# Silu by the hyperbolic tangent, joint splits of two heads, and other places for weight splits in the first attention

## The chip, the cores and the metric

The kernel runs on one core of a Trainium2 chip. The metric is the device time of one execution in microseconds (us), as the median of several. The engines are PE (TensorE, matrix products and transposes), DVE (VectorE), ACT (ScalarE), POOL (GpSimd) and SP (SyncE, which here only issues DMAs). Each engine runs its own instructions in program order, and semaphores order them between engines.

## What is computed

Two transformer blocks on 512 tokens of width 1024, all in float32. The change lies in the first block, whose core is this (projections by one matrix, two attentions with 8 heads each, gates by silu, an output projection and the sum with the input):

```python
proj = jnp.einsum('bsd,de->bse', xn, w_in[layer])
qa, ka, va, za, qi, ki, wi, qb, kb, vb, zb = jnp.split(proj, split_points, axis=-1)
...
a_out = dsa_attention(qa, ka, va, qi, ki, wi, bias_a)
b_out = dilated_attention(qb, kb, vb, bias_b)
mixed = jnp.concatenate([a_out.reshape(b, s, D_A) * jax.nn.silu(za),
                         b_out.reshape(b, s, D_B) * jax.nn.silu(zb)], axis=-1)
x = x + jnp.einsum('bse,ed->bsd', mixed, w_out[layer])
```

Attention a keeps, for each query, the best 128 keys of an index score; attention b is three dilated windows, here one causal softmax with a bias that counts how often a key is seen. The second block follows and isn't touched.

## The kernel before

Every float32 product is made of three products of halves: each operand is split into a high half (ACT copies it into a tile of type float32r, which rounds it) and a low half (the rest, by a subtraction on DVE or POOL), and PE adds high by high, high by low and low by high. So each operand passes through ACT and DVE before PE can use it.

The first attention is a loop over 64 steps, taken as pairs t, t+1. A step u is one token tile i (128 queries), one branch and one head; a group of 8 steps is two heads r = 0, 1 with i = 0, 1, 2, 3, branch b first (steps 0 to 31), then a (32 to 63). For the pair t, t+1 the engines do:

- PE: the scores of the pair (`pair1`, line 1086; at a group's start those of two pairs), then one or more chunks of the gate projection (`fill`), which are the other work of this stretch, then the transposes of the pair t-4 (`turn1`, line 1096), and at two places of each group the products with the values (`value1`, line 1111). Before each turn PE waits until the scores of the pair before are taken (`l_done`).
- DVE: `score1` (line 2269: bias, maximum, the score out of PSUM) for both steps, with a reciprocal of the sums of the pair before in between, which waits for that pair's exponentials; then, where a table says so, sums of values (`collect1`), the product of gate and attention (`mix`), the scaling of a finished gate tile (`gate_rows`), low halves of mixed rows (`mixed_low`), of gate weights (`low`, line 2090) and of output weights (`wo_low`); and last the low halves of the turned scores (`turned_low`, line 2222), which free the transpose bank (`t_free`).
- ACT: the high halves of the turned scores of the pair t-4 (`turned_high`, line 1761), the exponentials of the pair (`exps`, line 1578), low rows of the values' sums (line 1768), then the silus of two gate tiles (`silu`, line 1752), the high half of gate weights (`high`, line 1613), output weights (`wo_high`) and mixed rows (`mixed_high`), by the same kind of table.
- POOL: the scores times the reciprocal of their sum (line 2752), low halves of the values of branch a, the mask sums `combine` (line 2739), which `score1` needs in branch a, and a few low halves of output weights (line 2746).

The gate projection has eight tiles, zb 0 to 3 and za 0 to 3 (`FILL1`), with the weights in units F0 to F0+7 of 128x1024. A unit's raw weights have two places, so SP loads unit F0+2 only once PE has finished the tile F0, and so on. `HIGH1` and `LOW1` say at which step ACT and DVE split a unit: for F0+2 to F0+7 the high halves are at steps 10, 20, 28, 36, 43, 49, and the low ones at 12, 22, 30, 38, 44, 50; the low half of F0+1 is at step 1. `SILU_AT` has a pair of silus at steps 20, 36, 49 and 63. Two banks of PSUM take the transposes by turns (`t_bank`: tile n waits until tile n-2 is freed); each step is a tile of its own.

## Time and profile before

| | |
|---|---|
| median of 3 timed runs | 1031.36 us (1031.04 to 1031.43) |
| the profiled execution | 1029.16 us, of which 1027.3 us is the span from first to last instruction |
| granted TensorE clock | 0.999 of full speed |
| PE busy | 1005.7 us, 98% |
| DVE busy | 680.4 us, 66% |
| ACT busy | 563.2 us, 55% |
| POOL busy | 422.8 us, 41% |
| first attention | about 170 to 303 us of the span |

The profile is of one execution; its times are those of all rows below. An engine's rows give the start in the span, the length, the line of the kernel, and in brackets the idle time ahead of it with the instruction that ended it. A matmul's length runs past the start of the next, since they are pipelined. An engine is the bound where the others wait for it; idle time of others costs nothing by itself.

### The profile page before, as it was taken

To read this page: it belongs to the slowest core of one execution; us is meant where nothing else is said; L and a number is where in the kernel's file an instruction comes from. 1 tells how busy PE (TensorE), PEld (TensorE's weight loads), DVE (VectorE), ACT (ScalarE), POOL (GpSimd) and SP (SyncE) were. 2 spreads that over 40 slices of the span, in tenths; PEclk is the share of its full clock that TensorE was granted. 3 is DMA by queue.
4 is the path that set the end of the run, shared out by engine and by line. 5 is a ranking of instruction groups with operands and counts; after the bars stand their busy time and mean duration, and the time that the engine had idled before them with its cause. 6 is when DMAs were issued, how large, how long until landed. Compare 5 with 4: busy or idle time off the path is not lost. (4 is left out here: it accounts for less than half of the span.)

```text
span 1027.3 us, 14257 instructions
## 1 busy us (share of the span) xinstructions
PE 1005.7 (98%) x5150; PEld 826.2 (80%) x5150; DVE 680.4 (66%) x1207; ACT 563.2 (55%) x1032; POOL 422.8 (41%) x407
## 2 busy tenths in 40 slices
PE   9999999999989999999999999999999999999997
PEld 7788877777778898878887788888888888888885
DVE  5578997788974446824567879454322325999997
ACT  8455445778873355544567884234433446554564
POOL 0024011557840002900264430007779965874562
PEclk9999999999999999999999999999999999999999
DMA  9433321336140384233200362239999941443552
GB/s 336 104 98 109 88 67 36 83 83 191 56 175 1 103 267 143 60 82 83 63 2 1 121 229 62 82 111 323 347 352 349 356 168 62 153 143 135 205 185 82
DMA packets 100166, 146.25 MB, mean 142 GB/s; under 512 B 6480, under 2 KB 60496, under 8 KB 100096
## 3 DMA queue, kind: packets, MB, share of 16 engines
q1 hardware_dynamic: 86800, 130.75, 38.9%
q10 hardware_dynamic: 12768, 12.88, 4.0%
q0 software_dynamic: 528, 1.70, 0.9%
q8 instruction: 41, 0.67, 0.3%
q14 instruction: 29, 0.24, 0.1%
HBM read 123.69 MB, written 21.63 MB: 141 GB/s over the span
## 5 line engine op out<-in xcount | busy, mean ns | idle before, releaser
L2578 DVE TENSOR_TENSOR w_lo<-wring,w_hi 128x1024 fp32r<-128x1024 f32 x32 | 51.4, 1607 | 107.5 <-ACT w_hi L1944 107.5
L2090 DVE TENSOR_TENSOR u_lo<-wring,u_hi 128x1024 fp32r<-128x1024 f32 (+1 forms) x64 | 82.5, 1296 | 53.6 <-ACT u_hi L1613 52.9
L935 PE MATMUL bank<-u_hi,h_hi 128*128 128x512 f32 (+1 forms) x288 | 110.9, 385 | 0.1
L935 PE MATMUL bank<-u_hi,h_lo 128*128 128x512 f32 (+1 forms) x288 | 109.3, 379 | 0.0
L935 PE MATMUL bank<-u_lo,h_hi 128*128 128x512 f32 (+1 forms) x288 | 109.0, 378 | 0.0
L1613 ACT ACTIVATE u_hi<-wring 128x1024 fp32r<-128x1024 f32 (+1 forms) x64 | 66.2, 1034 | 69.4 <-PE bank L935 54.7
L935 PE MATMUL bank<-h_hi,w_hi 128*128 128x512 f32 (+2 forms) x272 | 103.2, 379 | 0.0
L935 PE MATMUL bank<-h_hi,w_lo 128*128 128x512 f32 (+2 forms) x272 | 103.1, 379 | 0.0
L935 PE MATMUL bank<-h_lo,w_hi 128*128 128x512 f32 (+2 forms) x272 | 103.1, 379 | 0.0
L935 PE MATMUL bank<-h_hi,u_hi 128*128 128x512 f32 x224 | 93.8, 419 | 0.4 <-ACT arena L1555 0.2
L1441 PE MATMUL bank<-s_hi,f_hi 128*128 128x512 f32 x224 | 87.4, 390 | 0.7 <-DVE f_lo L2612 0.7
L935 PE MATMUL bank<-h_lo,u_hi 128*128 128x512 f32 x224 | 87.7, 391 | 0.0
L935 PE MATMUL bank<-h_hi,u_lo 128*128 128x512 f32 x224 | 87.7, 391 | 0.0
L1442 PE MATMUL bank<-s_hi,f_lo 128*128 128x512 f32 x224 | 87.2, 389 | 0.0
L1443 PE MATMUL bank<-s_lo,f_hi 128*128 128x512 f32 x224 | 87.2, 389 | 0.0
L1944 ACT ACTIVATE w_hi<-wring 128x1024 fp32r<-128x1024 f32 x32 | 33.9, 1060 | 91.9 <-PE bank L935 91.9
L2804 POOL TENSOR_SCALAR arena<-arena,stats 128x128 f32<-128x128 f32 (+3 forms) x64 | 40.5, 642 | 95.0 <-DVE stats L2534 94.8
L2752 POOL TENSOR_SCALAR x<-x,stats 128x128 f32<-128x128 f32 (+3 forms) x64 | 49.4, 777 | 53.9 <-DVE stats L2277 53.9
L2604 DVE TENSOR_TENSOR s_lo<-wring,s_hi 128x2048 fp32r<-128x2048 f32 (+1 forms) x32 | 67.8, 2119 | 5.6 <-ACT s_hi L1974 5.6
L935 PEld LDWEIGHTS bank<-u_hi,h_hi 128*128 128x128 f32 x288 | 54.1, 188 | 11.5 <-issue 1.2
L935 PEld LDWEIGHTS bank<-u_lo,h_hi 128*128 128x128 f32 x288 | 54.1, 188 | 10.2
L1974 ACT ACTIVATE s_hi<-wring 128x2048 fp32r<-128x2048 f32 (+1 forms) x32 | 54.3, 1696 | 14.0 <-PE bank L1443 13.8
(382 smaller groups left out, 2600.2 us busy)
## 6 DMA issues: line engine op xcount, KB each, us to landing
wring<-in_w_in SPq DMA_DIRECT2D x60, 512.0 KB, 3.9
wring<-in_w_ff ACTq DMA_DIRECT2D x12, 1024.0 KB, 8.7
wring<-sums_kept SPq DMA_DIRECT2D x16, 768.0 KB, 4.2
wring<-in_w_ff SPq DMA_DIRECT2D x22, 512.0 KB, 6.2
wring<-in_w_ff SPq DMA_DIRECT2D x32, 256.0 KB, 3.3
sums_kept<-wring SPq DMA_DIRECT2D x22, 256.0 KB, 5.2
wring<-in_w_out SPq DMA_DIRECT2D x2, 2048.0 KB, 13.2
wring<-in_w_ff SPq DMA_DIRECT2D x4, 1024.0 KB, 6.9
```

Source lines behind the costliest of these rows:

```text
L935: last = mm(b, lhs, rhs, start=(start and n == 0), stop=(stop and n == 2))
L1441: mm(b, f[0][:, token], w[0][:, high], start=start, stop=False)
L1442: mm(b, f[1][:, token], w[0][:, high], start=False, stop=False)
L1443: return mm(b, f[0][:, token], w[1][:, lows], start=False, stop=stop)
L1613: run(u_hi[hi_place(u)][:, 0:unit_cols(u)], raw_unit(u), ACT.Copy).then_inc(u_hi_done, 1)
L1944: run(dst, src, ACT.Copy).then_inc(w_hi_done, 1)
L1974: run(s_hi[m % 4][:, 0:PAIR - at], pair_raw(m)[:, at:PAIR], ACT.Copy).then_inc(s_hi_done, 1)
L2090: v.tensor_tensor(u_lo[raw_place(u)][:, 0:cols], raw_unit(u), u_hi[hi_place(u)][:, 0:cols].bitcast(F32), ALU.subtract).then_inc(u_lo_done, 1)
L2578: v.tensor_tensor(cut(w_lo[ring3(m)]), src, cut(w_hi[ring3(m)]).bitcast(F32), ALU.subtract).then_inc(w_lo_done, 1)
L2604: v.tensor_tensor(s_lo[pair_place(m)][:, at:PAIR], pair_raw(m)[:, at:PAIR], s_hi[m % 4][:, 0:PAIR - at].bitcast(F32), ALU.subtract)
L2752: g.tensor_scalar(logits1[u % 8], logits1[u % 8], den[:, u:u + 1], unit_factor, ALU.mult, ALU.mult).then_inc(scaled, 1)
L2804: g.tensor_scalar(place, place, den2[:, u:u + 1], gates[:, i, at:at + 1], ALU.mult, ALU.mult).then_inc(scaled, 1)
```

## The change

The silu z * sigmoid(z) is written as 0.5 * z * (1 + tanh(z/2)). ACT makes tanh(z/2) (`half_tanh`), and in a second pass adds 1; POOL multiplies by z (`gated`); the factor 0.5 goes into DVE's product `mix`. The eight tiles are taken one by one (`TANH_AT`, `GATED_AT`) instead of in four pairs, and the exponential's table is loaded ahead of the attention. For token tiles 0 and 1 the turned scores of both heads lie in one bank and are split by one ACT and one DVE instruction (`turned_high_pair`, `turned_low_pair`), and such a pair counts as one tile of the two banks. The high halves of F0+2 to F0+7 are at steps 9, 19, 27, 35, 41, 47. The low halves of F0+1, F0+3, F0+4 and F0+6 are done in two parts at two steps. Some of DVE's `mix` are at other steps.

```diff
@@ -198,12 +198,14 @@
-    HIGH1 = {filled[tile] + 2: unit_of[tile] + 2 for tile in FILL1 if unit_of[tile] + 2 < U2}
-    LOW1 = {1: F0 + 1, **{step // 2 * 2 + 2: u for step, u in HIGH1.items()}}
+    HIGH1 = {filled[tile] // 2 * 2 + 1: unit_of[tile] + 2 for tile in FILL1 if unit_of[tile] + 2 < U2}
+    LOW1 = {4: (F0 + 1, 0), 6: (F0 + 1, 1), 10: (F0 + 2, None), 20: (F0 + 3, 0), 22: (F0 + 3, 1), 28: (F0 + 4, 0), 30: (F0 + 4, 1),
+            38: (F0 + 5, None), 42: (F0 + 6, 0), 46: (F0 + 6, 1), 50: (F0 + 7, None)}
...
-    SILU_AT = {min(filled[FILL1[2 * n + 1]] + 2, NS - 1) if n < 3 else NS - 1: n for n in range(4)}
-    MIX_AT = {22: 0, 24: 1, 38: 2, 40: 3, 50: 4, 56: 5, 64: 6}
+    TANH_AT = {10: 0, 20: 1, 28: 2, 36: 3, 42: 4, 48: 5, 54: 6, 60: 7}
+    GATED_AT = {12: 0, 21: 1, 29: 2, 37: 3, 45: 4, 53: 5, 61: 6, 62: 7}
+    MIX_AT = {18: 0, 32: 1, 34: 2, 40: 3, 50: 4, 56: 5, 64: 6}
...
-    T1 += [("pt", u) for u in range(NS)]
+    T1 += [("pt", u) for u in range(NS) if steps1[u][0] >= 2 or u % 2 == 1]
...
+    TT.update({("pt", u): TT[("pt", u + 1)] for u in range(0, NS, 2) if steps1[u][0] < 2})
...
+        pt1_both = {part: half(f"pt1_pair_{part}", 6 * P, ("wring", pt1_at[0, part, 0])) for part in ("hi", "lo")}
...
@@ -1091,10 +1112,11 @@
-                b = t_bank(("pt", u))
+                b, at = t_bank(("pt", u)), (i + 1) * P * (u % 2) if i < 2 else 0
...
-                last.then_inc(t_full, 1)
+                if i >= 2 or u % 2 == 1:
+                    last.then_inc(t_full, 1)
...
+                if g == "qa":
+                    nc.scalar.preload_act_table(ACT.Exp)
...
-            def silu(tile):
+            def half_tanh(tile):
                 act.wait_ge(a_free, AT[tile] + 1)
-                z = zT[:, (0 if tile[0] == "za" else 4) + tile[1], :]
-                run(z, z, ACT.Silu).then_inc(z_done, 1)
+                act.wait_ge(l_done, (0 if tile[0] == "zb" else HALF) + NH * (tile[1] + 1))
+                run(tanh_place(tile), gate_place(tile), ACT.Tanh, scale=0.5).then_inc(half_tanh_done, 1)
+                act.wait_ge(half_tanh_done, FILL1.index(tile) + 1)
+                run(tanh_place(tile), tanh_place(tile), ACT.Identity, bias=unit_factor).then_inc(tanh_done, 1)
+
+            def turned_high_pair(u):
+                i, o = steps1[u][0], u // NH
+                k = TT[("pt", u)]
+                act.wait_ge(t_full, k + 1)
+                if o >= 1:
+                    act.wait_ge(pv_done, 4 * (o - 1) + 2)
+                run(both_places("hi", i), pair_turned(k, i), ACT.Copy).then_inc(pt_hi_done, 2)
...
-                        for n in range(2):
-                            silu(FILL1[2 * SILU_AT[u] + n])
+                    if u in TANH_AT:
+                        half_tanh(FILL1[TANH_AT[u]])
...
+            def turned_low_pair(u):
+                i = steps1[u][0]
+                dve.wait_ge(pt_hi_done, u + 2)
+                v.tensor_tensor(both_places("lo", i), pair_turned(TT[("pt", u)], i), both_places("hi", i).bitcast(F32), ALU.subtract)\
+                    .then_inc(t_free, 1)
...
-                v.tensor_tensor(zT[:, k, cols], zT[:, k, cols], qk1[:, o // 4, o % 4, OUTS, cols], ALU.mult).then_inc(gated_done, 1)
+                v.scalar_tensor_tensor(zT[:, k, cols], zT[:, k, cols], 0.5, qk1[:, o // 4, o % 4, OUTS, cols], ALU.mult, ALU.mult)\
+                    .then_inc(gated_done, 1)
...
+            def gated(tile):
+                pool.wait_ge(tanh_done, FILL1.index(tile) + 1)
+                z = gate_place(tile)
+                g.tensor_tensor(z, z, tanh_place(tile), ALU.mult).then_inc(z_done, 1)
...
+                if u in GATED_AT:
+                    gated(FILL1[GATED_AT[u]])
```

The order on ACT around step 20, in the program before. `x,stats<-x,stats` is a pair of exponentials, `pt1_hi...` a turned copy, `arena<-arena` a silu, `u_hi3` the high half of unit F0+3:

```order
L1578 ACTIVATE x,stats<-x,stats 128x384 x2
L1752 ACT_TABLE_LOAD
L1752 ACTIVATE arena<-arena 128x512 x2
L1613 ACTIVATE u_hi3_90<-wring 128x1024
L1761 ACTIVATE pt1_hi00_118<-bank4 128x2x128
L1761 ACTIVATE pt1_hi01_119<-bank5 128x2x128
L1578 ACT_TABLE_LOAD
L1578 ACTIVATE x,stats<-x,stats 128x512 x2
```

The same place in the program after; line 1776 is the tanh, 1778 the second pass, 1754 a mixed high half:

```order
L1635 ACTIVATE u_hi3_90<-wring 128x1024
L1786 ACTIVATE pt1_pair_hi_118<-bank4 128x2x128
L1600 ACTIVATE x,stats<-x,stats 128x384 x2
L1776 ACTIVATE arena<-arena 128x512
L1778 ACTIVATE arena<-arena,stats 128x512
L1754 ACTIVATE qk1_half_103<-arena 128x512
L1786 ACTIVATE pt1_pair_hi_118<-bank5 128x2x2x128
L1600 ACTIVATE x,stats<-x,stats 128x512 x2
```

The loads are gone, one silu is two passes, the weights' high half stands a turn earlier, and the turned scores of a pair are one copy.

ACT around steps 40 to 43, before, where `u_hi2` is the high half of unit F0+6:

```order
L1761 ACTIVATE pt1_hi11_115<-bank5 128x3x128
L1578 ACTIVATE x,stats<-x,stats 128x128 x2
L1730 ACTIVATE qk1_half_103<-arena 128x512
L1761 ACTIVATE pt1_hi10_114<-bank4 128x4x128
L1761 ACTIVATE pt1_hi11_115<-bank5 128x4x128
L1578 ACTIVATE x,stats<-x,stats 128x256 x2
L1768 ACTIVATE consts<-bank6 64x512
L1613 ACTIVATE u_hi2_89<-wring 128x1024
```

And after:

```order
L1795 ACTIVATE pt1_hi11_115<-bank5 128x3x128
L1600 ACTIVATE x,stats<-x,stats 128x128 x2
L1635 ACTIVATE u_hi2_89<-wring 128x1024
L1795 ACTIVATE pt1_hi10_114<-bank4 128x4x128
L1795 ACTIVATE pt1_hi11_115<-bank5 128x4x128
L1600 ACTIVATE x,stats<-x,stats 128x256 x2
L1802 ACTIVATE consts<-bank6 64x512
L1776 ACTIVATE arena<-arena 128x512
```

The high half of F0+6, which waits for its DMA, has moved ahead of the turned copies of steps 38 and 39.

## Rows read from the trace of the kernel before

**Rows 1.** The page's first part: busy time, share of the span, instructions.

```profile
PE 1005.7 (98%) x5150; PEld 826.2 (80%) x5150; DVE 680.4 (66%) x1207; ACT 563.2 (55%) x1032; POOL 422.8 (41%) x407
```

**Rows 2.** Who PE waited for, 168 to 300 us: total, times, longest.

```profile
PE bank L1096 <- DVE pt_lo L2222: 4.5, 6, 1.3
PE bank L1086 <- DVE stats L2269: 3.9, 6, 1.4
```

**Rows 3.** Order of time, PE: start, length, instruction, idle before it.

```profile
175.24 0.79 PE L1086 MATMUL bank<-qk_half 64*128 64x384 f32 x6 [1.18 <-DVE stats L2269]
...
193.96 0.95 PE L1086 MATMUL bank<-qk_half 64*128 64x128 f32 x12 [0.71 <-DVE stats L2269]
...
209.83 0.85 PE L1096 MATMUL bank<-consts,x 128*128 128x128 f32 x6 [0.89 <-DVE pt_lo L2222]
...
214.18 1.09 PE L1096 MATMUL bank<-consts,x 128*128 128x128 f32 x8 [0.52 <-DVE pt_lo L2222]
...
244.75 1.10 PE L1096 MATMUL bank<-consts,x 128*128 128x128 f32 x8 [0.37 <-DVE pt_lo L2222]
...
248.09 0.38 PE L1096 MATMUL bank<-consts,x 128*128 128x128 f32 x2
...
254.81 0.96 PE L1086 MATMUL bank<-qk_half 64*128 64x128 f32 x12 [1.39 <-DVE stats L2269]
...
265.89 0.30 PE L1096 MATMUL bank<-consts,x 128*128 128x128 f32 x1 [1.05 <-DVE pt_lo L2222]
...
292.37 1.09 PE L1096 MATMUL bank<-consts,x 128*128 128x128 f32 x8 [1.35 <-DVE pt_lo L2222]
```

**Rows 4.** Order of time, ACT at step 20.

```profile
204.43 1.28 ACT L1752 ACT_TABLE_LOAD   x1
...
206.78 1.04 ACT L1613 ACTIVATE u_hi<-wring 128x1024 fp32r<-128x1024 f32 x1
...
208.38 1.28 ACT L1578 ACT_TABLE_LOAD   x1
```

**Rows 5.** Groups by line and shape, ACT, 168 to 300 us: count, busy, mean ns.

```profile
L1761 ACT ACTIVATE pt_hi<-bank 128x512 fp32r<-128x512 f32 x16 | 8.7, 593 | 11.8 <-PE bank L1096 11.8
...
L1761 ACT ACTIVATE pt_hi<-bank 128x256 fp32r<-128x256 f32 x16 | 5.2, 378 | 7.3 <-PE bank L1096 7.3
...
L1752 ACT ACT_TABLE_LOAD x4 | 5.1, 1283 | 0.1
...
L1752 ACT ACTIVATE arena<-arena 128x512 f32<-128x512 f32 x8 | 4.6, 624 | 0.0
```

**Rows 6.** Loads of units F0+2 and F0+6 (issue, then KB and us to landing), ACT beside them.

```profile
182.14 0.37 SPq L739 DMA_DIRECT2D wring<-in_w_in  x1
...
wring<-in_w_in SPq DMA_DIRECT2D x1, 512.0 KB, 4.6
...
186.23 1.09 ACT L1761 ACTIVATE pt_hi<-bank 128x512 fp32r<-128x512 f32 x2 [2.13 <-PE bank L1096]
...
240.75 0.42 SPq L739 DMA_DIRECT2D wring<-in_w_in  x1
...
wring<-in_w_in SPq DMA_DIRECT2D x1, 512.0 KB, 7.4
...
245.41 1.09 ACT L1761 ACTIVATE pt_hi<-bank 128x512 fp32r<-128x512 f32 x2 [1.47 <-PE bank L1096]
...
248.20 1.06 ACT L1613 ACTIVATE u_hi<-wring 128x1024 fp32r<-128x1024 f32 x1
```

**Rows 7.** POOL: a group by shape, two rows in time, busy time from 280 to 290.

```profile
L2739 POOL TENSOR_TENSOR junk<-arena,x 128x512 f32<-128x512 f32 x8 | 10.3, 1285 | 0.0
...
257.91 2.80 POOL L2752 TENSOR_SCALAR x<-x,stats 128x512 f32<-128x512 f32 x1
...
286.96 2.90 POOL L2752 TENSOR_SCALAR x<-x,stats 128x384 f32<-128x384 f32 x4
...
280.00:290.00 10.00, 9.04 (x61) 7.32 (x57) 7.53 (x22) 8.95 (x24) 9.51 (x12) 1.00 0.01 2
```

More of the change, by code:

```diff
@@ L444, in build, with both_places, pair_turned @@
         assert sum(pt1_size[key[0]] for key in pt1_at) == 5 * UNIT
-        pt1 = {key: half(f"pt1_{key[1]}{key[0]}{key[2]}", 2 * (2 * key[0] + 2) * P, ("wring", at)) for key, at in pt1_at.items()}
+        pt1 = {key: half(f"pt1_{key[1]}{key[0]}{key[2]}", 8 * P, ("wring", at)) for key, at in pt1_at.items() if key[0] == 1}
+        pt1_both = {part: half(f"pt1_pair_{part}", 6 * P, ("wring", pt1_at[0, part, 0])) for part in ("hi", "lo")}
+        pt1.update({(0, part, r): pt1_both[part][:, 3 * P * r:3 * P * (r + 1)] for part in pt1_both for r in range(2)})
+        pt1_pair = {part: both[:, :].rearrange("p (r m s) -> p r m s", r=2, s=P) for part, both in pt1_both.items()}
+        def both_places(part, i):
+            return pt1_pair[part][:, :, 1:2, :] if i == 0 else pt1_pair[part][:, :, 0:3:2, :]
+        def pair_turned(k, i):
+            return bank[4 + k % 2][:, 0:2 * (i + 1) * P].rearrange("p (r m s) -> p r m s", r=2, s=P)
         def turned_place(part, i, r):
@@ L453, in build, with gate_place, tanh_place @@
         mix_place = lambda k: (0, k - 4) if k >= 4 else (1, k)
+        def gate_place(tile):
+            return zT[:, (0 if tile[0] == "za" else 4) + tile[1], :]
+        def tanh_place(tile):
+            return qk1[:, 0 if tile[0] == "zb" else 1, tile[1], MIX_LO, :]
         def wo_raw(n, k, count=1):
@@ L555, in build @@
         ki_lo_done = sem("ki_lo_done")
+        half_tanh_done = sem("half_tanh_done")
+        tanh_done = sem("tanh_done")
         z_done = sem("z_done")
@@ L1093, in turn1 @@
                 pe.wait_ge(scaled, u + 1)
-                b = t_bank(("pt", u))
+                b, at = t_bank(("pt", u)), (i + 1) * P * (u % 2) if i < 2 else 0
                 for j in range(i + 1):
-                    last = nc.tensor.transpose(b[:, (i - j) * P:(i - j + 1) * P], logits1[u % 8][:, j * P:(j + 1) * P], ident)
-                last.then_inc(t_full, 1)
+                    last = nc.tensor.transpose(b[:, at + (i - j) * P:at + (i - j + 1) * P], logits1[u % 8][:, j * P:(j + 1) * P], ident)
+                if i >= 2 or u % 2 == 1:
+                    last.then_inc(t_full, 1)
             def value1(o, n, r):
@@ L1770, in _ @@
             for t in range(0, NS + 4, 2):
-                if t >= 4:
+                if t >= 4 and steps1[t - 4][0] < 2:
+                    turned_high_pair(t - 4)
+                elif t >= 4:
                     turned_high(t - 4)
@@ L2084, in head_low, with low @@
                                        small[:, gain:gain + 1], place[:, :, hi, :].bitcast(F32), ALU.mult, ALU.subtract).then_inc(t_free, 1)
-            def low(u):
+            def low(u, part=None):
                 dve.wait_ge(u_hi_done, u + 1)
-                cols = unit_cols(u)
-                v.tensor_tensor(u_lo[raw_place(u)][:, 0:cols], raw_unit(u),
-                                u_hi[hi_place(u)][:, 0:cols].bitcast(F32), ALU.subtract).then_inc(u_lo_done, 1)
+                size = unit_cols(u) // (1 if part is None else 2)
+                cols = slice((part or 0) * size, (part or 0) * size + size)
+                done = v.tensor_tensor(u_lo[raw_place(u)][:, cols], raw_unit(u)[:, cols],
+                                       u_hi[hi_place(u)][:, cols].bitcast(F32), ALU.subtract)
+                if part != 0:
+                    done.then_inc(u_lo_done, 1)
             def branch_low(e):
@@ L2298, in _ @@
                     if u in LOW1:
-                        low(LOW1[u])
+                        low(*LOW1[u])
                     if WO_HIGH.get(u - 2, 5) < 5:
                         wo_low(WO_HIGH[u - 2])
-                if t >= 4:
+                if t >= 4 and steps1[t - 4][0] < 2:
+                    turned_low_pair(t - 4)
+                elif t >= 4:
                     turned_low(t - 4)
@@ L2747, in output_low @@
                     .then_inc(wo_lo_done, 1)
+            def gated(tile):
+                pool.wait_ge(tanh_done, FILL1.index(tile) + 1)
+                z = gate_place(tile)
+                g.tensor_tensor(z, z, tanh_place(tile), ALU.mult).then_inc(z_done, 1)
             for u in range(NS):
```

2 lines of the change are left out of this document (removed).

## The prediction

> **What bounds the kernel now.** The page first: PE is busy 98% of the span [rows 1], so only time in which PE stands still, or is fed late, can be won, and the change touches nothing but the first attention (170 to 303 us). Next, who PE waits for in that stretch. Two entries lead: the transposes (line 1096) wait for the low split of an earlier turned tile, 4.5 us, and the score products (line 1086) for the score step of DVE, 3.9 us [rows 2]. Then the order of time on PE: rows 3 has the stalls, the time in brackets being the stall. I number the work by the step u of the loop (a pair t, t+1 per turn). They are, in order: the scores of step 4 (1.18) and of step 16 (0.71), the transposes of steps 20 (0.89), 22 (0.52) and 38 (0.37), the scores of step 48 (1.39), the transposes of step 48 (1.05) and of step 62 (1.35). The row without a stall, at 248.09, is the transposes of step 40.
>
> Last, what ACT does ahead of them [rows 4]. At step 20 it loads a table, runs two silus, makes a high half of a weight tile, splits step 18, and loads the exponential's table again: 204.43 to 209.66, 5.2 us, where the loads alone are 2.6. PE's stall at 209.83 is the far end of it: the transposes need a bank that DVE's low split frees, and that split comes behind ACT's copy and DVE's own low half of the weights. So PE is the bound, and ACT and DVE, in turns, set its gaps.
>
> **The change, part by part.** Times below are in the coordinates of the trace of before; "+x" is how much later than there PE stands.
>
> *Tables.* Line 1752 has four loads of 1283 ns [rows 5], and line 1578 as many, one of them at the very start and one behind each of the first three silu pairs [rows 4]. The program after has none between the exponentials and one before the attention, where ACT waits for PE anyway: 8 x 1.28 = 10.3 us leave ACT in this stretch. Added are eight Identity passes (about 0.62 to 0.7 us, from a silu's 624 ns [rows 5]) = 5.3 us, so ACT gets 5.0 us back. POOL gets eight products of 128x512; its 128x512 sum takes 1285 ns [rows 7], so 10.3 us.
>
> A load stands right behind the instruction before it and the next right behind it, 1.28 us in all [rows 4]. The Trainium skill, "ScalarE: Activation LUTs", section "What ACT_TABLE_LOAD costs", gives 1283 ns and another 1380 ns of drain, 2.66 us per switch. The first half agrees with the trace; the drain isn't seen in it. By that rule ACT would get 21.3 us instead of 10.3; I take the row.
>
> *Joint splits.* For 16 pairs (token tiles 0 and 1) two copies of ACT become one. Two copies of 128x256 take 2 x 378 ns, one of 128x512 593 ns [rows 5]: 0.16 us less for each of 8 pairs. The 128-wide pairs, not shown, I put at as much (bounds 0 and 0.4). DVE's halves shrink likewise. More useful is that a pair takes one transpose bank, so the first head of the next pair waits for a split that is one pair older.
>
> *Step 4.* The 1.18 us wait is for scores 3, behind the reciprocal which waits for ACT's exponentials (late by one load), and behind a whole low half. Both go: no load, and the low half is now at steps 4 and 6, where DVE stood waiting for ACT. The next thing, ACT's two exponentials, ends before PE asks. -1.2.
>
> *Steps 8 to 16.* The high half of the third gate tile (u_hi for step unit F0+2) moves from the turn of step 10 to that of step 8. Its DMA is issued at 182.14 and lands 4.6 us later, at 186.74 [rows 6]. ACT reaches the place at 184.1, so it now stands in front of the turned copies of step 6, which began at 186.23 [rows 6]; they begin at 186.74 + 1.05 = 187.8. DVE does the low half to 189.0, then the splits of 6 and 7 to 189.65 and 190.3. PE wants the first one's bank at 188.77: 0.9 lost. On the other side the low half, which stood ahead of the splits of step 8 and the scores of 14 and 15 and caused most of the 0.71 at step 16, is gone from there. Following ACT (copies, exponentials, low rows, tanh and Identity, joint copy, exponentials) the scores of step 15 end at 194.2 and PE goes on at 194.35 instead of 193.96. +0.4 (bounds -0.5 and +1.5).
>
> *Step 20.* ACT: the high half now comes one turn earlier, its DMA has landed by then (asked for 4 us before, and nothing else in flight). Exponentials end at 205.6, tanh, Identity and a mixed-high copy at 207.45, joint copy of step 18 at 208.0, instead of 208.37. DVE holds only half of a low half and one mixed-low there and frees the bank at 209.45; PE wants it at 209.2 for its second head. PE stands at 209.2 instead of 209.83, from +0.4 to -0.6: -1.0.
>
> *Steps 22 to 26.* The 0.52 us came from the same backlog, and so did, by my reading, 0.6 in the value products and scores right behind (the same rows stand that much closer together in the groups before): -1.1 (bounds -0.5 and -1.2). What stays is a wait of 0.2 to 0.3 at each group's start, where scores need a whole turn from PE to DVE and back.
>
> Up to step 32 PE is then 2.9 us ahead, and nothing in the rows stops it till step 38.
>
> *Steps 38 to 48, the seventh gate tile.* This is the term that decides. The 0.37 at step 38 goes (ACT is 1 us ahead there). But the high half of unit F0+6 moves from step 43 to step 41. Its load is queued behind eight strip loads and two megabyte loads; it is issued at 240.75 and takes 7.4 us: 248.15 [rows 6]. Before, ACT came to it at 248.20, so it had no slack at all [rows 6]. Now ACT comes to it at 242.3 and stands 5.8 us; queued behind it are the turned copies of step 38, which ran at 245.41 [rows 6]. All of this chain hangs on PE's own progress, so the gain so far moves the landing as well. High half to 249.2, copies to 250.25; DVE's split of 38 to 250.5 (a half low half is ahead of it); PE's transposes of step 40, which ran at 248.09 [rows 3], start at 250.55: +2.45. From there: score 47 at 256.25 (its mask sum on POOL at 255.45), PE goes on at step 48 at 256.35 instead of 254.81 [rows 3]. The 1.39 wait of before is inside that, so the net is +1.6 (bounds 0 and +3.5: the landing is uncertain by one, and one more megabyte load is now issued some 1 us earlier beside it).
>
> *Steps 48 to 53.* ACT has two weight copies of 128x1024, the high half of the last tile, whose DMA, issued at 255.2 by this walk, lands by 259.8 at the price of the third tile's, and then the turned copies: they end at 262.4, DVE's at 263.95. PE loses 0.4, 0.6 and 0.95 (1.95) where it lost 1.35 before, the 1.05 and 0.30 on the pair's second head; since its products behind close up again, I take +0.3 (bounds 0 and +0.6). *Steps 54 to 56*: POOL's chain of scale and mask sum waits for a reciprocal 0.3 later: +0.3.
>
> *The end.* The last silus stood ahead of the splits of steps 60 to 63 (PE's 1.35). They go, but POOL now has two products between the scalings of steps 61, 62 and 63, and it is in one piece there: scalings from 286.96 to 289.82 [rows 7]. With 2 x 1.29 more the last scaling ends at 292.4, and PE wants it about 291.4 for the second head. 1.0 stays of the 1.35 and a smaller wait of 0.5 behind it: -0.8.
>
> **Sum:** -1.2 + 0.4 - 1.0 - 1.1 + 1.6 + 0.3 + 0.3 - 0.8 = -1.5 us. The profiled execution took 1029.16 us, 1027.30 of it span; it is 2.2 below the median of the three timed runs, 1031.36. A difference of PE time carries over to either, so I forecast 1031.36 - 1.5 = 1029.9 us.
>
> **Rivals.** *A, the seventh tile doesn't hold ACT* (its load lands by 243 to 244, since what is ahead in the queues is gone by then). For it: the third tile's load took 4.6 us [rows 6]. Against it: this one took 7.4 with the same company. Then 0.4 at step 38, 1.2 of the 1.39 and 1.3 of the 1.35 at step 48 go too: -2.9 - 0.4 - 1.2 - 1.3 - 0.8 = -6.6, and 0.4 in the value products behind step 62: -7.0, 1024.4 us.
>
> *B, POOL becomes the pacemaker and it gets slower.* One 128x512 scaling, 0.77 elsewhere, took 2.80 us at 257.91 while DVE subtracted two weight tiles [rows 7], and between 280 and 290 POOL was busy 9.51 of 10 us [rows 7]. If the products of steps 53, 61 and 62, where it has no room, take 2.8 instead of 1.29, that is 3 x 1.5 = 4.5 us more in front of PE: 1029.9 + 4.5 = 1034.4. It decides from about 2.5 us per product (3 x 1.2 = 3.6: 2.1 over the time of before). Against it: the mean of the mask sums, the same shape, was 1.285 [rows 7]. The Trainium skill, "SBUF — State Buffer", section "Who interferes with whom", has a DVE instruction with two SBUF inputs and a GpSimd one that reads SBUF block each other for a whole instruction; the 2.80 agrees with that.
>
> *C, the gain isn't there*: PE's gaps close but it waits for scores instead, each turn of PE and DVE being near its own limit; 1031.4, within 1 either way. For it: the wait at each group's start, which no part of the change shortens.
>
> **How the numbers follow.** Forecast case 0.58, with a spread of about 2 us from its bounds: 0.24 below -2.1, 0.32 within, 0.02 above. A 0.18, B 0.16, C 0.08 (0.05 of it within, 0.03 slower, if the waits for scores are longer than the gaps). A measurement of this kernel tells about 0.2% (2.1 us) from no change. Faster by over 0.2%: 0.24 + 0.18 = 0.42. Slower: 0.02 + 0.16 + 0.03 = 0.21. Within: 0.37. Range 1024.4 to 1033.6; it cuts off the far half of A and of B. Both signs hold much, so the likeliest case alone: 1027.5 to 1031.5.
>
> **What would show it.** On PE: no stall at step 4; transposes of steps 20 to 22 without one; a stall of 2 to 3 us at step 40's transposes, and ahead of it ACT idle some 5 us, released by a DMA into wring, before line 1635. If that idle is under 1 us, A is right. A second, shorter one of that kind (2.5 us) at step 8. If POOL's products (line 2799) average over 2 us and PE's stalls move to the scaled tiles from step 45 on, B. I'm wrong altogether if the landing of the seventh tile moves, or if ACT's copies overtake it.

## The result, and the profile after

The change made the kernel slower. In nine runs each, the kernel after has a median of 1037.20 us (1033.90 to 1039.78), the kernel before 1031.43 (1031.03 to 1034.08); the ratio is 1.0044, 95% interval 1.003 to 1.0058. On another chip (e12 below) it was 1.003 (1.0017 to 1.0042). I had forecast 1029.9 in a range of 1024.4 to 1033.6. The profiled execution took 1034.49 us, 1032.7 of it span: 5.4 us longer than before, and 5.05 of that is there when the first attention ends. The nine runs fall in two groups: four of 1033.90 to 1034.49, three of them with a granted clock of 0.998 over the span and one with 0.995, and five of 1037.20 to 1039.78 with 0.993 to 0.995. The profile is of the first group; none was taken of the second, so where its clock fell isn't known.

The page's first part, which answers to [rows 1]:

```profile
PE 1007.4 (98%) x5150; PEld 827.8 (80%) x5150; DVE 681.1 (66%) x1195; ACT 559.7 (54%) x1017; POOL 437.0 (42%) x415
```

Who PE waited for from 168 to 306 us, which answers to [rows 2] (total, times, longest):

```profile
PE bank L1117 <- DVE pt_lo L2266: 5.2, 4, 1.9
PE bank L1117 <- DVE pt_pair_lo L2259: 3.5, 3, 1.7
PE bank L1107 <- DVE stats L2314: 1.5, 4, 0.7
PE bank L956 <- DVE u_lo L2126: 1.4, 1, 1.4
```

The work did shift as intended: ACT is 3.5 us less busy, POOL 14.2 more. The waits for scores are down from 3.9 us to 1.5, but those of the transposes (line 1117, which was 1096) rose from 4.5 to 8.7: 5.2 for single low splits and 3.5 for joint ones (line 2259), and there is a new one for gate weights (line 2126). In order of time on PE, which answers to [rows 3]:

```profile
174.43 0.79 PE L1107 MATMUL bank<-qk_half 64*128 64x384 f32 x6
...
189.00 0.42 PE L1117 MATMUL bank<-consts,x 128*128 128x128 f32 x2 [0.76 <-DVE pt_lo L2266]
...
210.84 0.52 PE L1117 MATMUL bank<-consts,x 128*128 128x128 f32 x3 [1.73 <-DVE pt_pair_lo L2259]
...
240.99 0.52 PE L1117 MATMUL bank<-consts,x 128*128 128x128 f32 x3 [1.02 <-DVE pt_pair_lo L2259]
...
249.75 0.42 PE L1117 MATMUL bank<-consts,x 128*128 128x128 f32 x2 [1.38 <-DVE pt_lo L2266]
...
255.76 0.96 PE L1107 MATMUL bank<-qk_half 64*128 64x128 f32 x12 [0.73 <-DVE stats L2314]
...
258.11 0.50 PE L956 MATMUL bank<-h_hi,u_hi 128*128 128x512 f32 x1 [1.39 <-DVE u_lo L2126]
...
296.07 1.09 PE L1117 MATMUL bank<-consts,x 128*128 128x128 f32 x8 [1.90 <-DVE pt_lo L2266]
```

The stall at step 4 is gone (174.43). Four places are new or worse. The first two are transposes of a pair's second head, at step 20 (210.84) and step 36 (240.99). This is what DVE and POOL did ahead of them:

```profile
207.65 1.29 POOL L2799 TENSOR_TENSOR arena<-arena 128x512 f32<-128x512 f32 x1
...
207.75 1.74 DVE L2299 TENSOR_TENSOR qk_half<-arena,qk_half 128x512 fp32r<-128x512 f32 x1 [0.88 <-ACT qk_half L1754]
...
237.43 1.73 POOL L2799 TENSOR_TENSOR arena<-arena 128x512 f32<-128x512 f32 x1
...
237.93 2.32 DVE L2126 TENSOR_TENSOR u_lo<-wring,u_hi 128x1024 fp32r<-128x1024 f32 x1
```

DVE's mixed-low took 1.74 us, and ended 0.55 behind the end of POOL's product (208.94); the same subtraction takes 0.69 elsewhere. The low half of unit F0+5 took 2.32 instead of 1.21 (e3 below, which has no such product beside it). The same happens once more ahead of the 1.39 at 258.11, with the product of step 45 and the second part of the low half of F0+6:

```profile
256.23 1.27 POOL L2799 TENSOR_TENSOR arena<-arena 128x512 f32<-128x512 f32 x1
...
256.29 1.76 DVE L2126 TENSOR_TENSOR u_lo<-wring,u_hi 128x512 fp32r<-128x512 f32 x1
```

This subtraction of 128x512 takes 0.68 in e3, and PE doesn't wait behind it there. Third, ACT stands in front of the high half of F0+6, and later in front of the last tanh:

```profile
247.21 1.06 ACT L1635 ACTIVATE u_hi<-wring 128x1024 fp32r<-128x1024 f32 x1 [4.40 <-DMA wring<-in_w_in]
...
288.79 0.63 ACT L1776 ACTIVATE arena<-arena 128x512 f32<-128x512 f32 x1 [2.12 <-DVE stats L2314]
```

Fourth, behind the stall of 1.90, the granted clock. In each row of the windows: the window and its length in us, busy time (count) of PE, PEld (PE's weight loads), DVE, ACT, POOL, then the granted clock as a share of 2.4 GHz, the DMA share and GB/s.

```profile
294.00:296.00 2.00, 0.17 (x1) 0.00 (x0) 1.97 (x4) 0.71 (x2) 2.00 (x2) 1.00 0.00 0
296.00:298.00 2.00, 1.60 (x10) 1.32 (x11) 1.95 (x5) 1.26 (x3) 1.92 (x3) 0.98 0.00 0
298.00:300.00 2.00, 2.00 (x10) 1.72 (x8) 2.00 (x4) 1.69 (x4) 1.47 (x2) 0.50 0.68 244
300.00:302.00 2.00, 2.00 (x12) 1.95 (x12) 1.47 (x2) 0.14 (x1) 0.59 (x1) 0.66 1.03 414
```

PE had 0.17 us of work in 294 to 296, and from 298 it ran at half clock (1.2 GHz) for over 3 us. The kernel before has 1.00 in this stretch. e3 (below) has the same wait for the last tanh and keeps its clock at 1.00, and it loses 1.7 there instead of 2.8; it also has next to no products, so at most some 1.1 of the 2.8 goes with the clock.

**Where the time went.** For each kernel, PE's start of the same instruction less that in the trace of before, as the change in each stretch. The stretches end, in the time of before, at the scores of step 4 (175), the scores of step 16 (194), the value products behind step 22 (218), the transposes of step 38 (245), fill products behind step 48 (259), score products at 280, and the end of the attention (303). An offset of 0.3 to 3.2 us that each execution brings along from ahead of the attention is taken off. Each row is one profiled execution; the medians of the timed runs stand with the experiments. "half" marks a stretch with the clock at half in part. The experiments of the later rows follow below.

```
                    to 175  194   218   245   259       280   303       sum
predicted            -1.2  +0.4  -2.1   0    +1.6      +0.6  -0.8      -1.5
after                -1.2  +0.5  -0.2  +0.8  +2.2      -0.2  +2.8 half +4.6
e12 after again      -1.2  +0.3  -0.3  +0.8  +3.8 half -1.8  +2.5 half +4.0
e1 late tanh         -1.2  +0.3  -2.1  +0.7  +5.2 half +1.0  +0.2      +4.1
e2 F0+6 back         -1.2  +0.3  -0.4  +0.7  +0.1      -0.2  +2.8 half +2.2
e3 no product        -1.3  +0.5  -2.2  -0.4  +4.4 half +1.4  +1.7      +4.1
e4 late, F0+6 back   -1.2  +0.4  -0.2  +0.7  +0.1      -0.2  +0.2      -0.1
e5 product at 23     -1.3  +0.2  -1.4  +0.8  +1.7 half -1.7  +0.2      -1.6
e6 F0+2 back         -1.2  +0.2  -2.1  +0.7  +1.8 half -1.8  +1.7 half -0.8
e7 old silus         -1.3  +0.2  +0.2  +0.3  +0.1      +0.3  +0.2      +0.1
e8 joint only         0.0  +0.1  -0.3   0.0   0.0       0.0  +0.2      +0.1
e9 e6, product at 23 -1.2  +0.2  -2.1  +0.7  +0.2      -0.2  +1.7 half -0.7
e10 low F0+5 split   -1.3  +0.2  -1.5  -0.1  +1.7 half -1.8  +1.7 half -1.0
e11 end reordered    -1.3  +0.2  -2.1  -0.1  +0.1      -0.1  -0.1      -3.4
```

### The profile page after: what moved, and what is told of

Its sections match the earlier page's. It is cut to its first block and busy times, and to the rows that moved or that the text cites. A ratio compares the mean times of both kernels' runs of the same rounds, so it can differ in the third digit from the quotient of the medians.

```text
span 1032.7 us, 14234 instructions
## 1 busy us (share of the span) xinstructions
PE 1007.4 (98%) x5150; PEld 827.8 (80%) x5150; DVE 681.1 (66%) x1195; ACT 559.7 (54%) x1017; POOL 437.0 (42%) x415
## 5 line engine op out<-in xcount | busy, mean ns | idle before, releaser
L2126 DVE TENSOR_TENSOR u_lo<-wring,u_hi 128x1024 fp32r<-128x1024 f32 (+2 forms) x68 | 85.0, 1257 | 57.5 <-ACT u_hi L1635 56.8
L956 PEld LDWEIGHTS bank<-u_hi,h_lo 128*128 128x128 f32 x288 | 54.1, 188 | 9.3
```

The costliest lines, as they stand in the source:

```text
L956: last = mm(b, lhs, rhs, start=(start and n == 0), stop=(stop and n == 2))
L2126: done = v.tensor_tensor(u_lo[raw_place(u)][:, cols], raw_unit(u)[:, cols], u_hi[hi_place(u)][:, cols].bitcast(F32), ALU.subtract)
```

## The experiments

The ratios are to the kernel before on the same chip, with 95% intervals; each batch of four (e1 to e4, e5 to e8, e9 to e12) shared a chip. The kernel after ran on the chip of the last batch alone, so what is said of e1 to e8 against it, and of kernels of different batches against each other, compares ratios across chips.

### e1, e2 and e4: the two largest losses

e1 moves the last tanh behind the last exponentials:

```diff
-    TANH_AT = {..., 54: 6, 60: 7}
-    GATED_AT = {..., 53: 5, 61: 6, 62: 7}
+    TANH_AT = {..., 54: 6, 62: 7}
+    GATED_AT = {..., 53: 5, 61: 6, 63: 7}
```

> The changed kernel with one edit: the tanh of the last gate tile and its second pass at step 62 instead of 60 (behind the exponentials of steps 62 and 63), its product on POOL at step 63 instead of 62. The changed kernel lost 5.4 us of span, about 2.9 of it behind 280 us: ACT stood 2.12 us there because this tanh waits until all scores are taken. Theory 1 (this wait starves PE, and PE's clock falls to half behind it): ACT's idle time ahead of line 1776 goes, the transposes of step 62 wait under 1 us, the granted clock stays at 1.00 from 290 to 303, and the drift of PE against the kernel before at the end of the attention falls from 5.05 to about 2.2; median 1033.7 to 1034.7, and no run above 1036 if the spread of the changed kernel's runs (1033.9 to 1039.8) came from this place. Rival (POOL's two products at the end are what holds PE): POOL has the same work, so PE waits as long for the scaled scores; within 0.5 us of the changed kernel.

e2 puts the seventh gate tile's weights back:

```diff
+    HIGH1[43] = HIGH1.pop(41)
...
-    LOW1 = {..., 42: (F0 + 6, 0), 46: (F0 + 6, 1), 50: (F0 + 7, None)}
+    LOW1 = {..., 44: (F0 + 6, None), 50: (F0 + 7, None)}
```

> The changed kernel with the seventh gate tile's weights as before: high half of unit F0+6 at step 43 instead of 41, low half whole at step 44 instead of in two parts at 42 and 46. Theory 1 (the early high half held ACT 4.4 us for its DMA, cost PE 1.4 at the transposes of step 40 and, through the late second low part, 1.39 at 258.11): both PE stalls go, the drift of PE at 270 us falls from about +2.0 to between 0 and +0.5; time 1.5 to 2.3 us below the changed kernel, if nothing later eats it. Rival (the wait of 1.39 for the scores of step 48 takes both in, as in the kernel before): 0.5 us or less below. The clock fall at 297 to 301 stays in either.

e4 is both edits together.

> The edits of the two kernels above together: last tanh at step 62, its product at 63, and the seventh gate tile's weights as before. Theory 1 (two separate places): the gains add, 4.3 to 5 us below the changed kernel in its profile, so about 1031 to 1032.5, level with the kernel before. Rival (the places are not independent: what is won at 258 is waited for again at the end): the gain is that of the first alone, some 2.8 us, 1033.5 or more.

**Measured:** before 1030.71; e1 1031.79, ratio 1.0008 (0.9993 to 1.0024); e2 1031.71, 1.0005 (0.9993 to 1.0017); e4 1029.40, 0.9984 (0.9972 to 0.9996). Against the kernel after (1.0044, 1.003) each edit alone wins 2 to 4 us, and both together 5 to 6: theory 1 holds for both places. In the profiles e4 is 4.7 us below the kernel after, which is the 2.6 that e1 wins in the last stretch and the 2.1 that e2 wins before 259; by the medians the sum of the single gains is 5 to 8, so there they add up only roughly.

In e1's profile (1033.25 us, in the upper part of its runs of 1028.91 to 1036.20) the last stretch costs 0.2 us instead of 2.8, and the clock stays at 1.00 there; the transposes of step 62 wait 0.40. But one part of the expectation missed: a run above 1036 was left (1036.20). The clock can fall at the other gap too, and in this profile all but 0.5 us of what e1 wins at the end and at step 20 is lost there. e1's ACT and PE around the high half of F0+6, in order of time:

```profile
246.82 1.06 ACT L1635 ACTIVATE u_hi<-wring 128x1024 fp32r<-128x1024 f32 x1 [6.03 <-DMA wring<-in_w_in]
...
249.35 0.66 PE L1117 MATMUL bank<-consts,x 128*128 128x128 f32 x2 [2.99 <-DVE pt_lo L2266]
```

And its windows (columns as above):

```profile
246.00:248.00 2.00, 0.36 (x2) 0.00 (x0) 0.09 (x1) 1.18 (x2) 0.20 (x1) 1.00 0.47 171
248.00:250.00 2.00, 0.65 (x3) 0.68 (x4) 2.00 (x4) 1.98 (x7) 0.00 (x0) 0.61 0.03 11
250.00:252.00 2.00, 2.00 (x12) 2.00 (x11) 1.56 (x7) 1.97 (x4) 1.55 (x2) 0.50 0.00 0
252.00:254.00 2.00, 2.00 (x11) 1.68 (x12) 1.03 (x2) 1.81 (x6) 2.00 (x3) 0.50 0.00 0
254.00:256.00 2.00, 2.00 (x10) 1.22 (x7) 0.86 (x4) 0.00 (x0) 0.55 (x1) 0.69 0.00 0
```

PE was 2.0 us earlier here than in the kernel after (transposes of step 38 at 243.02 instead of 245.03), yet those of step 40 start at 249.35 instead of 249.75. The load lands at 246.8 instead of 247.2. Its issue in the kernel after, then in e1:

```profile
240.51 0.42 SPq L760 DMA_DIRECT2D wring<-in_w_in  x1
```

```profile
239.34 0.42 SPq L760 DMA_DIRECT2D wring<-in_w_in  x1
```

It was issued 1.2 us earlier and took 7.5 us instead of 6.7; the DMA share is 0.98 to 1.19 in every window from 236 to 246, with strips and megabyte loads issued ahead of it. That doesn't make the landing fixed. With each execution's offset taken off, it comes at 246.8 in the kernel after, 246.5 in e12, 246.2 in e1, 245.3 in e3, and 244.5 to 245.0 in e6, e9 and e11, whose PE is as far ahead as e1's at 236 (3.1 us against 3.0; 0.9 in the kernel after). Over the fourteen profiles the landing is about 1 us earlier for each us that PE is ahead there, with a scatter of 0.6, and the load takes 6.5 to 8.1 us. So e1 had the slower load of the two: by the same count PE is 2.2 us ahead of the kernel after at step 38, the landing 0.6, and 1.6 of the lead is waited away in front of step 40. The longer gap then brings the clock down. In e2 ACT comes to the tile at 249.05, 0.9 us behind its landing, with no wait at all, and the stretch costs 0.1 instead of 2.2.

The end of e4 shows what is next there, a low half of the output weights that POOL makes behind the last product:

```profile
292.22 1.09 PE L1117 MATMUL bank<-consts,x 128*128 128x128 f32 x8 [0.41 <-DVE pt_lo L2266]
294.86 0.70 PE L956 MATMUL bank<-za_half,qk_half 128*128 128x512 f32 x2 [1.54 <-POOL qk_half L2793]
```

### e3, e5, e6, e9: POOL's products, and a race at step 20

e3 takes nearly all of the products away. It leaves out 510 of the 512 columns of each, so its gates are not the right ones; it is for the time alone:

```diff
-                g.tensor_tensor(z, z, tanh_place(tile), ALU.mult).then_inc(z_done, 1)
+                g.tensor_tensor(z[:, 0:2], z[:, 0:2], tanh_place(tile)[:, 0:2], ALU.mult).then_inc(z_done, 1)
```

> The changed kernel, but POOL multiplies only two of the 512 columns of each gate tile (line 2799 as 128x2 instead of 128x512), so most of the gate isn't multiplied by z. All waits stay. Theory 2 (a POOL product beside a DVE subtraction makes both longer, and the joint splits come late behind it): DVE's mixed-low at step 20, 1.74 us in the changed kernel, takes about 0.7, its low half of F0+5, 2.32, about 1.2; the stalls of 1.73 at step 20 and 1.02 at step 36 fall below 0.5 and the 1.39 at 258.11 shrinks; with POOL free at the end too the time falls by 3 to 5 us. Rival (ACT's second pass and its queue are the cause, DVE would wait for ACT anyway): the two stalls stay at over 1 us, and at most 1.5 us is won, at the end only.

**Measured:** 1035.34, ratio 1.0034 (1.0021 to 1.0046). By the ratios it is 1 us better than the kernel after was in its first series, and no better than in e12; 3 to 5 were expected. The collisions do go (F0+5's low half takes 1.21; the stretches to 218 and 245 win 2.0 and 1.2), and so does the wait of 1.39 for the gate weights:

```profile
257.35 0.68 DVE L2126 TENSOR_TENSOR u_lo<-wring,u_hi 128x512 fp32r<-128x512 f32 x1
```

But all of it is lost in front of F0+6's load: ACT waits 6.15 us there, PE 3.11, and the clock falls from 249 to 255. So the products cost 3.2 us up to step 38 and over 1 behind it, and without them the total is hardly better as long as F0+6 is split early. POOL as pacemaker (rival B) is out. What the products cost in a kernel with F0+6 at its old place wasn't run.

e3 alone doesn't show that the product costs PE time at step 20, though. e1 has the full products and shows the same gain there. Its DVE and POOL rows there:

```profile
206.29 2.25 POOL L2804 TENSOR_SCALAR x<-x,stats 128x384 f32<-128x384 f32 x2 [2.54 <-DVE stats L2322]
...
206.73 0.77 DVE L2299 TENSOR_TENSOR qk_half<-arena,qk_half 128x512 fp32r<-128x512 f32 x1
```

It is a race. If ACT's mixed-high is there when DVE has taken its scores, DVE goes first: its mixed-low takes 0.77, and POOL's two scalings are held (2.25 instead of 1.30). If DVE has to wait for ACT (0.88 in the kernel after), POOL's scalings and then its product come in between, and one of DVE's next two subtractions is held until the product ends: the mixed-low (1.74 and 1.87 in after and e4) or the low half behind it (1.77 in e12 and e2, where the mixed-low takes 0.83 and 0.79). With the product at step 21 PE lost 1.9, 1.7, 1.7 and 1.9 us (after, e12, e2, e4) or nothing (e1, e6) at the transposes of step 20, counted from the first head's start to the second's against the 0.33 us of a kernel without a stall. What seems to decide it stands a turn earlier, at the high half of unit F0+3, which the change put at step 19. In the kernels that lost, ACT waited there for its load (the kernel after, then e1):

```profile
203.24 1.06 ACT L1635 ACTIVATE u_hi<-wring 128x1024 fp32r<-128x1024 f32 x1 [0.79 <-DMA wring<-in_w_in]
```

```profile
202.26 1.04 ACT L1635 ACTIVATE u_hi<-wring 128x1024 fp32r<-128x1024 f32 x1
```

It is 0.79, 0.45, 0.50 and 0.68 us in after, e12, e2 and e4, where the load took 4.9 to 5.3 us, and nothing in e1 and e6, where it took 3.7 and 3.8. Of the kernels without a product at 21, e3, e9 and e11 had no such wait and lost nothing, e5 waited 0.59 and lost 0.6, and e10 is the exception: no wait, and yet DVE stood 0.22 us for ACT and PE lost 0.5. This is a correlation over eleven profiles; the high half of F0+3 alone wasn't moved.

e5 is e4 with the product moved:

```diff
-    GATED_AT = {12: 0, 21: 1, ...}
+    GATED_AT = {12: 0, 23: 1, ...}
```

> The kernel of e4_late_f6 with one number changed: POOL's product of the second gate tile at step 23 instead of 21. In e4_late_f6 this product (208.23 to 209.52) ran beside DVE's mixed-low of step 20, which took 1.87 us instead of 0.7, and PE lost 1.9 us at the transposes of step 20. Theory (a POOL product and a DVE subtraction of two SBUF operands take turns, and it is this collision that PE pays): the mixed-low takes 0.7 to 0.8, PE loses less than 0.9 there, and the time is 1.0 to 1.9 us below e4_late_f6 (ratio to the kernel before 0.9965 to 0.9975). Rival (DVE waits for ACT's mixed-high there anyway, 0.74 us, and POOL's scaled scores collide in the product's place): PE loses 1.5 us or more as before, and the time is within 0.4 us of e4_late_f6.

**Measured:** before 1031.01; e5 1028.87, ratio 0.9978 (0.9968 to 0.9987), 0.6 us better than e4 within overlapping intervals. The mixed-low takes 0.69 and PE loses 0.6 at step 20 instead of 1.9, as the theory had it; in its rows DVE stands 0.65 us for ACT there, which accounts for the 0.6. The time is between theory and rival, and its profile holds a clock fall at 255 that e4's doesn't. In four kernels with the product at 23 the loss was 0.6, 0, 0.5 and 0 (e5, e9, e10, e11), never 1.7.

e6 is e4 with the third gate tile's weights put back:

```diff
+    HIGH1[10] = HIGH1.pop(9)
-    LOW1 = {..., 10: (F0 + 2, None), ...}
+    LOW1 = {..., 12: (F0 + 2, None), ...}
```

> The kernel of e4_late_f6 with the third gate tile's weights as in the kernel before: high half of unit F0+2 at step 10 instead of 9, low half at 12 instead of 10. By the prediction's sum the early place costs 0.4 net: the stall of 0.66 at the transposes of step 8 goes (drift there 0.9 lower), and 0.5 of the wait at the scores of step 16 comes back; so 0.4 us below e4_late_f6 (0 to 0.8). Rival (the later place pushes ACT's and DVE's work of step 12 into the next turn): a stall of over 0.7 at step 16 or at 12's transposes, 0.3 us or more above it.

**Measured:** 1027.86, ratio 0.9974 (0.9964 to 0.9984): 1.0 us better than e4 by the ratios, within overlapping intervals, where I had put 0.4. The stall at step 8 is gone, and from step 4 to 16 it loses 0.2 instead of 0.4. The larger part, 1.9 at step 20 in its profile, is the race going the good way. Whether the later place of F0+2 makes that likelier I can't tell from one profile.

e9 is e6 with the product at 23.

> The kernel of e6_f2_back (last tanh at 62, the weights of the third and the seventh gate tile as in the kernel before) with POOL's product of the second gate tile at step 23 instead of 21. Reading so far: at step 20 POOL's scaled scores and product and DVE's mixed-low race for the same port; in the profile of e6_f2_back DVE came first and PE lost nothing there, so the later product can win nothing in such an execution. Theory (a race that goes one way or the other from one execution to the next): the profile shows the mixed-low at 0.7 to 0.8 and PE's loss at step 20 under 0.9 whichever comes first; median 0 to 0.7 us below e6_f2_back, 0.9970 (0.9963 to 0.9976) of the kernel before. Rival (the product at 23 meets other work of DVE): above 0.9978.

**Measured:** before 1031.07; e9 1028.81, ratio 0.9975 (0.9963 to 0.9987), the same as e6: the smallest gain that was expected, nothing where the race was won anyway.

### e7 and e8: the parts alone

e7 is e4 with the silus of the kernel before, in pairs at steps 20, 36, 49 and 63, and `mix` as it was.

> The kernel of e4_late_f6 with the silus of the kernel before: pairs by the silu table at steps 20, 36, 49 and 63, no second pass, no product on POOL, a plain product on DVE, and the products with the attention at the steps of before; joint splits and the places of the weight halves stay those of e4_late_f6. Theory (what the tables give back, the products on POOL take: 1.9 us at step 20 and 1.3 at step 36 lost to collisions): within 1 us of e4_late_f6, and PE's stalls at steps 20 to 22 are those of the kernel before (0.89 and 0.52) less what the joint splits and the earlier high half save. Rival (the table loads are the gain, as the prediction had it with 2.1 us at steps 20 to 26 and 0.8 at the end): 2 to 3 us above e4_late_f6, slower than the kernel before.

e8 has nothing of the change but the joint splits.

> The kernel before with the joint splits alone: the turned scores of both heads of token tiles 0 and 1 in one bank, split by one ACT and one DVE instruction; silus, tables and all weight halves as before. Theory (a pair takes one transpose bank, so the next pair waits for an older split): the stalls of 0.89 at step 20 and 1.35 at step 62 shrink by 0.3 to 0.5 each, 0.5 to 1.2 us below the kernel before. Rival (the bank of a pair is free only when both heads are split, so the second head waits longer): the stalls stay or grow, within 0.3 us of the kernel before or above it.

**Measured:** e7 1031.23, ratio 1.0001 (0.999 to 1.0012); e8 1031.40, 1.0002 (0.9992 to 1.0012). The joint splits alone give nothing, as the rival had it. In e8 the stall at step 20 moved from the first head (0.89 before) to the second:

```profile
209.37 0.49 PE L1117 MATMUL bank<-consts,x 128*128 128x128 f32 x3
210.69 0.52 PE L1117 MATMUL bank<-consts,x 128*128 128x128 f32 x3 [0.83 <-DVE pt_pair_lo L2259]
```

e7 is 1.7 us above e4 by the ratios, between theory and rival. Its profile says why: the stretch from step 16 to 22 costs +0.2 with the tables, and -2.1 with the tanh when the race is won, -0.2 when it is lost. So the silus by tanh (no loads, one tile at a time, other places for `mix`) are worth the 2.1 us that I had put there, and the product's collision can take nearly all of it. Which of the three gives it, e7 doesn't separate.

### e10 to e12: the better version, and the kernel after once more

```diff
-    LOW1 = {..., 38: (F0 + 5, None), ...}
+    LOW1 = {..., 36: (F0 + 5, 0), 38: (F0 + 5, 1), ...}
```

> The kernel of e9_f2_23 with the low half of unit F0+5 in two parts at steps 36 and 38 instead of whole at 38, where it took 2.3 us beside POOL's product and PE lost 1.2 at the transposes of step 38's turn. Theory: the part at 38 ends about 0.6 earlier, so the stall on the joint low split (L2259) near 241 shrinks from 1.26 to about 0.6; 0.5 to 0.7 us below e9_f2_23, part of it taken back by the scores' wait of step 48 (1.82). Rival (POOL's product holds DVE till it ends, whatever stands there): the stall stays above 1.0, nothing won.

**Measured:** 1027.21, ratio 0.9958 (0.9944 to 0.9972). The stretch to step 38 goes from +0.7 to -0.1 and the stall there is gone, a little more than expected (0.5 to 0.7); that the ratio is 1.7 us better than e9's is within overlapping intervals.

e11, on top of it:

```diff
-    WO_POOL = {59: 5, 63: 6}
+    WO_POOL = {59: 5}
...
                 if t == NS + 2:
                     collect1(GROUPS - 2)
-                    mix(7, slice(0, S // 2))
...
+                if t == NS - 2:
+                    dve.wait_ge(wo_lo_done, 6)
+                    wo_low(6)
+            mix(7, slice(0, S // 2))
             mixed_low(6)
```

> The kernel of e10_low5_split with two moves at the end of the attention: the low half of output weight 6 from POOL (behind the last product) to DVE at step 62, and DVE's first product of the last gate tile behind the splits of steps 62 and 63. In the kernels with the late tanh PE waits 1.54 us for that low half on POOL at the end. Theory (POOL's queue of two products and two low halves is what the last silu's table was before): this wait goes, the next one is that for the turned low split at about 0.5 us; 1.0 to 1.5 us below e10_low5_split, and fewer runs in which the clock falls behind it. Rival (DVE is as late with its splits as POOL with the weights): 0.4 us or less.

**Measured:** 1027.38, ratio 0.9964 (0.9953 to 0.9975). In the profile the 1.54 wait is gone, waits of 0.84 and 0.57 stand in its place, and the last stretch costs -0.1 instead of +0.2 (or +1.7 where the clock falls). The 1.0 to 1.5 us below e10 that were expected don't show: in time it isn't distinguishable from e10; e10's five runs against e11's twelve can't settle a microsecond. Both beat the kernel before by 3.7 to 4.3 us, and the kernel after, on the same chip (e12), by some 7.

> The changed kernel once more, on the chip of these runs. Theory: at the median 1.0044 (1.003 to 1.006) of the kernel before, with the same holding of ACT by the load of unit F0+6 (4 to 6.2 us) in its profile. What may differ from one execution to another is the collision at step 20 (mixed-low of DVE 0.75 or 1.75 us) and at which gap the granted clock falls to half (about 250 us, or 298 us, or both): spans fall into groups some 2 us apart. Rival (the collision and the clock's falls are fixed by the program): the profile shows the same rows of 1.74 and 1.73 at step 20 and the clock at half only from 297 to 301.

**Measured:** 1034.45 (1032.54 to 1037.56), ratio 1.003 (1.0017 to 1.0042), the low end of what was expected. ACT stands 4.46 us in front of F0+6, and PE's stalls are those of the first profile. The clock falls twice, near 260 and near 298. So the theory holds for the clock, which differs from run to run. The race at step 20 was lost as in the first profile, PE's loss is 1.7; here it was not the mixed-low that was held (0.83) but DVE's next subtraction (1.77). That it differs between executions rests on e1: its program is that of the kernel after up to step 40, as those of e2, e4 and e12 are, and it alone won the race.

## Why the prediction was wrong

Forecast and profile differ by 6.1 us in this attention (-1.5 and +4.6). The end is 3.6 of it, steps 20 to 26 are 1.9, step 36 is 0.8 and steps 38 to 48 are 0.6; steps 48 to 56 came out 0.8 better. Point by point, with the table above:

- **Step 4, -1.2:** right, -1.2 in each kernel that has it.
- **Steps 8 to 16, +0.4:** right, +0.5; ACT stood 2.54 us for the load of F0+2.
- **Joint splits:** two copies of 128x256 cost ACT 0.66 us together in its rows before (285.98), since they overlap, and not 2 x 378 ns; the joint one takes 0.58. So the saving for a pair is 0.08, not 0.16, and e8 found nothing in time.
- **Steps 20 to 26, -2.1:** the mechanism and the size were right, and it is there in e1, e6, e9 and e11. Two steps failed. "Its DMA has landed by then" held in only some executions; the load was issued at 197.94 and took 5.28 us in the kernel after, right behind eight strip loads of the bias issued from 193.64 to 197.2 (DMA share 0.61 from 196 to 198), so "nothing else in flight" didn't hold. ACT waited up to 0.79 us for F0+3, and so DVE for ACT. And "frees the bank at 209.45": DVE's mixed-low was costed at its undisturbed length. I had quoted, for rival B, that DVE and POOL hold each other up, and applied it only to POOL's products getting longer. They stayed at 1.40 on average (11.2 us for eight), under B's 2.5; it was DVE that got longer. The Trainium skill, "SBUF — State Buffer", section "Who interferes with whom", has it for both engines: "Issue order, not op shape, decides who blocks." The rows agree: DVE 1.74 where POOL was first, POOL 2.25 where DVE was.
- **"Nothing in the rows stops it till step 38":** wrong by 0.8 at step 36, by the same collision with the product at 37 (e3, which has no such product, gains 0.4 there, so the collision is worth 1.2).
- **Steps 38 to 48, +1.6:** the mechanism was right: ACT idle 4.40 us before line 1635, released by the DMA, and PE's transposes at 249.75, where I had 250.55. Their stall was 1.38, not 2 to 3, since PE came to them without the 2.9 us that I had given it. The total of the stretch was +2.2. One thing was missed: the second part of F0+6's low half, at step 46, cost 1.39 at 258.11, because beside the product of step 45 it took 1.76 us instead of 0.68, the same unpriced collision a third time. "The gain so far moves the landing as well" holds in the main (about 1 us for each us over fourteen profiles), but the load's own time varies by 1.6 us, and what PE gains once the load is issued is waited away in front of it.
- **Steps 48 to 56, +0.6:** -0.2.
- **The end, -0.8:** wrong in sign, +2.8. I had costed the tanh and its product, and not the wait that comes with them. The tanh is written where keys of the scores lie, so it waits until all 64 scores are taken. At step 60 ACT stands 2.12 us for scores 62 and 63, and behind it are queued a weight copy, the joint copy of step 58 (290.60, before 285.98), and the exponentials of 62 and 63. In e1 the stretch costs +0.2. At most some 1.1 of the 2.8 goes with the clock at half, by e3's 1.7 at full clock.
- **The rivals:** A didn't happen (4.40 us of idle, not under 1); B not, as said; C not, since the gaps didn't close. The loss came from two mechanisms that no rival named: DVE held by POOL's products (B had only the reverse), and the wait that came with the last tanh's new place. The range failed for the same reason, and because no term held the price of a clock fall.

## What to carry to other kernels

When work gets a new place to write to, read what must be finished before it may write there, and count that wait with all that is queued behind it on the engine. A product given to a less busy engine isn't free if the two hold each other up: price both of them at their held length, and give the product a slot in which the engine on the path waits or reads from a bank (e5's product at step 23, beside the turned low splits, took 1.30, and the splits their usual 1.02). An instruction that waits for a load holds all that is queued behind it on its engine: put it where the load has landed with room for its scatter (6.5 to 8.1 us here), or what is won just ahead of it is waited away.

## What the hardware showed

TensorE's clock falls to half behind a gap, though not each time. At the scores of step 48 seven kernels (e2, e4, e5, e6, e9, e10, e11) have the same wait of 1.82 us, and the clock falls behind it in three (e5, e6, e10). First e4, then e5:

```profile
254.00:256.00 2.00, 0.22 (x4) 0.22 (x5) 2.00 (x8) 1.51 (x4) 0.77 (x2) 1.00 0.65 174
256.00:258.00 2.00, 2.00 (x18) 1.64 (x17) 1.99 (x10) 1.98 (x4) 2.00 (x3) 1.00 0.70 186
```

```profile
252.00:254.00 2.00, 0.23 (x4) 0.23 (x6) 2.00 (x8) 1.52 (x4) 0.77 (x2) 1.00 0.65 167
254.00:256.00 2.00, 2.00 (x15) 1.61 (x14) 1.99 (x10) 1.98 (x4) 2.00 (x3) 0.63 0.71 192
256.00:258.00 2.00, 2.00 (x7) 1.51 (x7) 1.57 (x2) 2.00 (x3) 2.00 (x2) 0.51 0.41 105
```

The one keeps 2.4 GHz, the other runs at 1.2 GHz for over 3 us. What it costs depends on what follows. Behind step 48 it is 1.6 us, and PE's later waits shrink by 1.5, so nearly all is given back by 280 (e5, e6 and e10: +1.7 or +1.8, then -1.7 or -1.8). At the end, with nothing but PE's own work behind it, 1.5 us stay (e9 and e10 +1.7, e4 and e5 +0.2, with the same waits of PE). After the longest gaps, 3 us in e1 and e3, it fell both times, for over 5 us. That the runs of the kernel after spread over 6 us fits this: the slower five have the lower granted clocks. No profile shows one of them.
